# Twelve input projections between the memory's and the samples' attentions, in one program with a ring

## What is computed

```python
z = rmsnorm(x, norm_mix) @ w_in           # 6936 columns: 54 units of 128, and 24 for gates
o_lru = lru_branch(lru_x, lru_gate, ...)  # convolution, gates, recurrence over the tokens
o_nsa = nsa_attend(q, ...)                # compressed, selected and window keys, gated
o_mem = mem_attend(mq, mkv)               # softmax(mq mk / sqrt(128)) mv, 4 heads, 256 rows
z = merge0*(o_lru @ w_up_a) + merge1*(o_nsa @ w_up_b) + merge2*(o_mem @ w_up_m)
h = x + z @ w_o
y = h + (silu(f @ w_ffn_gate) * (f @ w_ffn_up)) @ w_ffn_down    # f = rmsnorm(h)
```

## Time and profile before

| | us |
|---|---|
| median of 3 runs (2675.41 to 2675.78) | 2675.66 |
| the profiled execution, device time | 2671.46 |
| its span, first to last instruction | 2669.8 |
| TensorE busy | 2416.7 (91%) |
| VectorE, ScalarE, GpSimd busy | 1072.0, 724.7, 655.0 |

### The profile page before, as it was taken

One profiled execution on the slowest core, in us unless ns is written; L12 is line 12 of the kernel. 1 busy time (PEld: TensorE's weight loads), 2 busy tenths in 40 slices (PEclk: granted clock), 3 DMA queues, 4 the chain that ended last, 5 costly groups with the idle time before them and its releaser, 6 DMA issues. The chain is left out here.

```text
span 2669.8 us, 37831 instructions
## 1 busy us (share of the span) xinstructions
PE 2416.7 (91%) x14415; PEld 2234.0 (84%) x14415; DVE 1072.0 (40%) x1945; ACT 724.7 (27%) x1319; POOL 655.0 (25%) x399
## 2 busy tenths in 40 slices
PE   7996877989989899899856587999999999999999
PEld 7995647789888788799733577999999999999999
DVE  5465014436255564655433003263333333333333
ACT  5222011242352544644332004232211111111111
POOL 2212001111111011010035001234444434433443
PEclk9997789999999899999678568999999999999999
DMA  5224424224233221110056626332111111111112
GB/s 178 88 80 168 125 72 147 67 67 128 64 97 88 74 63 52 60 49 28 6 125 181 160 65 246 104 119 91 61 48 47 40 47 47 47 39 47 47 47 79
DMA packets 136151, 226.26 MB, mean 85 GB/s; under 512 B 29418, under 2 KB 95098, under 8 KB 135420
## 3 DMA queue, kind: packets, MB, share of 16 engines
q1 hardware_dynamic: 122492, 194.57, 23.5%
q0 software_dynamic: 6560, 25.22, 3.2%
q10 hardware_dynamic: 6976, 4.79, 0.7%
HBM read 176.80 MB, written 55.08 MB: 87 GB/s over the span
## 5 line engine op out<-in xcount | busy, mean ns | idle before, releaser
L1101 PE MATMUL att_facc<-h_hi,att_w_hi 128*128 128x344 f32 x960 | 337.7, 352 | 57.8 <-DVE att_zf L1281 44.5
L2153 PE MATMUL tl_acc<-tl_x_hi,tl_w_hi 128*128 128x344 f32 x1632 | 348.0, 322 | 21.1 <-DVE tl_x_lo L2216 14.0
L2153 PE MATMUL tl_acc<-tl_x_lo,tl_w_hi 128*128 128x344 f32 x1632 | 347.2, 321 | 0.0
L2153 PE MATMUL tl_acc<-tl_x_hi,tl_w_lo 128*128 128x344 f32 x1632 | 345.4, 320 | 0.0
L1101 PE MATMUL att_facc<-h_lo,att_w_hi 128*128 128x344 f32 x960 | 314.5, 328 | 0.0
L1101 PE MATMUL att_facc<-h_hi,att_w_lo 128*128 128x344 f32 x960 | 314.2, 327 | 0.0
L2153 PEld LDWEIGHTS tl_acc<-tl_x_hi,tl_w_hi 128*128 128x128 f32 x1632 | 275.2, 189 | 22.5 <-issue 15.9
L2153 PEld LDWEIGHTS tl_acc<-tl_x_lo,tl_w_hi 128*128 128x128 f32 x1632 | 277.0, 189 | 0.0
L2153 PEld LDWEIGHTS tl_acc<-tl_x_hi,tl_w_lo 128*128 128x128 f32 x1632 | 272.6, 188 | 0.0
L2118 POOL TENSOR_TENSOR tl_w_lo<-tl_raw,tl_w_hi 128x1024 fp32r<-128x1024 f32 x64 | 153.9, 2404 | 425.1 <-ACT tl_w_hi L2059 425.1
L1101 PEld LDWEIGHTS att_facc<-h_hi,att_w_hi 128*128 128x128 f32 x960 | 187.7, 196 | 72.4 <-DVE att_zf L1281 42.2
(11 more groups left out here) (355 smaller groups left out, 4031.5 us busy)
## 6 DMA issues: line engine op xcount, KB each, us to landing
tl_raw<-in_w_ff SPq DMA_DIRECT2D x66, 512.0 KB, 3.6
z<-att_zf SPq DMA_DIRECT2D x120, 172.0 KB, 3.7
att_raw<-in_w_in SPq DMA_DIRECT2D x40, 512.0 KB, 4.3
tl_tmp<-z SPq DMA_DIRECT2D x24, 516.0 KB, 4.4
tl_raw<-in_w_up SPq DMA_DIRECT2D x16, 512.0 KB, 4.0
fr_raw<-in_w_in SPq DMA_DIRECT2D x14, 512.0 KB, 4.8
zn<-fr_x SPq DMA_DIRECT2D x10, 516.0 KB, 2.9
fr_x<-in_xT SPq DMA_DIRECT2D x8, 644.0 KB, 10.3
```

The lines of the kernel that those rows point to most:

```text
L1101: mm = pe.matmul(facc[:, 0:CW], w[:, u % 2, k, :], h[:, k, c * CW:(c + 1) * CW], start=(x == 0), stop=(x == 23))
L2153: mm = pe.matmul(a[:, c, 0:CW], wt[:, s, k, :], x[:, x0, c * CW:(c + 1) * CW], start=first and n == 0, stop=last and n == 2)
```

## The change

Twelve of the 24 `merge` units (42 to 53) leave the attention. Their 144 ticks are dealt among the items of a new program, `memory_and_samples`, that replaces the block of the three parts. The first two of them have their weights loaded and split at the end of the attention's order. The products of the samples' memory move: its scores stand between the group product and the transposes of the samples' attention, its values at the end. All keys and values of the samples come through one ring of ten slots of 512 KB, filled by the sync queue alone; weights of the twelve units and stores of their chunks go through GpSimd's queue. The 24 copies to the outputs move into the attention (items 24 to 47), on GpSimd's queue. The loops of the memory's attention become straight code, and the two products of new and compressed keys become one.

The diff, cut to its core:

```diff
+FILL = 12
 def attention_and_recurrence(...)
-    UNITS += list(range(U_MG, NU_IN))
-    NU = len(UNITS)
+    NU = len(UNITS) + NU_IN - FILL - U_MG
+    UNITS += list(range(U_MG, NU_IN - FILL + 2))
-    TICKS = ((4,),) * 3 + ((2, 2, 2, 1, 1) * 4 + (2,) * 4,) * (QT - 3)
+    TICKS = ((3, 2),) * 3 + ((2, 1, 1, 1),) * (QT - 3)
...
+                if 0 <= J - COPY < len(copies):
+                    dst, src, slow = copies[J - COPY]
+                    pool.dma_start(dst, src, allow_slow_non_contiguous=slow).then_inc(c_out, 16)
...
+def memory_and_samples(nc, d, per, h_hi, h_lo, fill):
+    DEAL = {"begin": 4, "mat": 2, "ks": 3, "grp": 2, "km": 1, "turn": 2, "vs": 3, "vm": 2}
...
+    ITEMS = []
+    for b in range(0, NS, 2):
+        ITEMS += [("ks", b), ("ks", b + 1), ("kw", b)]
+    ITEMS += [("km", b) for b in range(NS)]
+    for b in range(0, NS, 2):
+        ITEMS += [("vs", b), ("vs", b + 1), ("vw", b)]
+    ITEMS += [("vm", b) for b in range(NS)]
...
+            def ring_load(i):          # sync queue
+                kind, b = ITEMS[i]
+                slot, landed = ring[:, i % NR], r_in[i % NR]
+                if i >= NR:
+                    was, of = ITEMS[i - NR]
+                    read = {"k": mk_mm if was == "km" else k_mm, "v": mo_mm if was == "vm" else o_mm}[was[0]]
+                    sp.wait_ge(read, of + (2 if was[1] == "w" else 1))
+                if kind in ("ks", "vs"):
...
+                    with sp.Fori(0, PAGES) as x:
+                        page = sp.value_load(pt[0:1, bass.ds(x + b * PAGES, 1)], ...)
+                        sp.dma_start(slot..., src[bass.ds(page, 1)]...).then_inc(landed, 16)
...
+            for m in range(QT):
+                constants(m)
+                for i in range(loaded, min(NR, loaded + 2)):
+                    ring_load(i)
+                    loaded += 1
+                if m >= 2:
+                    o_store(m - 2)
+                if m + 2 < QT:
+                    q_load(m + 2)
+            o_store(QT - 2)
+            o_store(QT - 1)
+            for i in range(loaded, len(ITEMS)):
+                ring_load(i)
...
+            filler(("begin", 0))       # TensorE
+            pe.wait_ge(m_in, 32)
             scores(0)
             for j in range(NJ):
...
                 turn(j)
+                filler(("mat", j))
...
+            for b in range(NS):
+                sample_scores(b)
+                filler(("ks", b))
+            pe.wait_ge(s_oe, NJ)
+            pe.wait_ge(g_mm, 1)
+            pe.matmul(S5[0:RW, 0:NCMP], grp[:], lc[:, 0:NCMP], ...).then_inc(tp_done, 1)
+            filler(("grp", 0))
...
+            for b in range(NS):
+                memory_scores(b)
+                filler(("km", b))
+            pe.wait_ge(w_done, 1)
...
+            filler(("turn", 0))
+            pe.wait_ge(te_done, 4)
...
+            for b in range(NS):
+                sample_values(b)
+                filler(("vs", b))
...
+            for b in range(NS):
+                memory_values(b)
+                filler(("vm", b))
```

More of the change, by code:

```diff
@@ L1007, in _ @@
             q_low(0, 0)
-            for u in range(2, NU):
+            for u in range(2, NU + 2):
                 if unit_at[u - 2] == -1:
@@ new lines, in _, with filler @@
+        @block.tensor
+        def _(pe):
+            def filler(p):
+                for tick in ticks[p]:
+                    u, c, g, x0 = tick // 12, tick // 4 % 3, tick // 4, 6 * (tick % 4)
+                    if tick % 12 == 0 and u >= 2:
+                        pe.wait_ge(f_lo, u - 1)
+                    if x0 == 0 and g:
+                        pe.wait_ge(f_ev, g)
+                    for x in range(x0, x0 + 6):
+                        k = x // 3
+                        w, h = ((w_hi, h_hi), (w_hi, h_lo), (w_lo, h_hi))[x % 3]
+                        mm = pe.matmul(facc[:, 0:CW], w[:, u % 2, k, :], h[:, k, c * CW:(c + 1) * CW],
+                                       start=(x == 0), stop=(x == 23))
+                    if x0 == 18:
+                        mm.then_inc(f_mm, 1)
@@ new lines, in memory_queries @@
+            def memory_queries(part):
+                if part == 0:
+                    chain(dve.memset(mqb[:], 0.0))
+                    dve.wait_ge(mc_in, 16)
+                q0 = mqb[:].rearrange("p n c -> p (n c)")
+                for x in range(8 * part, 8 * part + 8):
+                    ins = dve.tensor_copy(q0[:, x * (RP + 1):x * (RP + 1) + 1], mqs[:, x % MH, x // MH:x // MH + 1])
+                if part == 3:
+                    ins.then_inc(mqb_done, 1)
+            evict(("begin", 0))
@@ new lines, in _ @@
+                if j:
+                    evict(("mat", j - 1))
+                if j == 16:
+                    sample_queries()
+                if j in (18, 20, 22, 24):
+                    memory_queries((j - 18) // 2)
+            evict(("mat", NJ - 1))
+            for b in range(NS - 1):
+                evict(("ks", b))
+            dve.wait_ge(k_mm, NS)
+            dve.wait_ge(b_in, 16 * 2 * NS)
+            chain(dve.tensor_copy(lc[:, 0:40], S3[0:RW, 2:42]))
+            chain(dve.tensor_tensor(lc[:, 40:NCMP], S3[0:RW, 42:2 + NCMP], b_cmp[:], ALU.add))
@@ new lines, in _ @@
+            dve.wait_ge(me_done, 1)
+            chain(dve.reciprocal(msc[:, 3:4], msc[:, 2:3]))
+            dve.tensor_scalar(mpr[:], mpr[:], msc[:, 3:4], None, ALU.mult).then_inc(mp_done, 1)
+            for b in range(NS):
+                evict(("vs", b))
+            dve.wait_ge(o_mm, NS)
+            for g in range(G):
+                rows = slice(g * HD, (g + 1) * HD)
+                dve.tensor_copy(soT[rows], S0[rows, 0:RW].rearrange("p (b h) -> p h b", h=8)[:, g * R:(g + 1) * R, :]).then_inc(o_done, 1)
```

786 lines of the change are left out of this document (391 added, 395 removed).

## The result

The changed kernel takes 2739.8 us against 2675.7: slower by 2.4% (ratio 1.0245, 95% interval 1.0208 to 1.0283). The prediction was 2666. Its profiled execution took 2735.85 us, with a span of 2734.2.

The account below looks back on a forecast made before the run. TensorE was taken to bound the prompt's attention, with holes in the stages behind it; -104 us there and +94 us in the second program give -10 us, from 2675.7 to 2666 us. Own range 2650 to 2684; with rivals 2635 to 2702.

Parts of the forecast that it names:

- The sum's sign: Whole kernel: attention -104 us plus second program +94 us gives -10 us, a faster kernel.
- The price of a removed tick: Attention: 108 ticks at 1.04 us and 40 at 1.15 us leave, giving back 112 and 46 us.
- the borders: Attention: 33 chunks ending in the middle of an item each wait 0.94 us for the eviction, 31 us.
- What comes back in waits: Attention: 31 us at chunk borders plus 21 us (10 for the recurrence's blocks, 11 for the next four tiles) return.
- The copies: Attention: the 24 copies to the outputs hide on GpSimd's queue and cost nothing.
- Memory's attention: Second program: 142.6 us instead of 76.5, +66 us, 18 of them waits for query tiles on the sync queue.
- Samples' scores, chain, first values: Second program: from the end of the memory's attention at 1490.4 us to the first values at 1572.8 us.
- Values: Samples' values: the sync queue is the bound at 24.9 us a pair of sequences; 86.7 us for the stage.
- rival 1: Second program: the gathers cost nothing on the sync queue, kernel 2617 us; chance 0.13.
- rival 2: Samples' values: the clock stays low, a pair takes 26.9 us and TensorE is the bound, kernel 2696 us; chance 0.22.
- Memory's values and the way into the tail: End of second program: 32.0 us for the memory's values with their ticks, then 16.3 us to the tail.
- Rival 3: Attention: more comes back, through a lower clock or late VectorE; gain only 78 us, kernel 2692 us; chance 0.22.

Follow-up runs that it names:

- e1: The changed kernel with ticks in the first three query tiles dealt so every chunk ends with its item: 2721.5 us, ratio 1.0162.
- e7: e6 with ticks 2, 1, 1 instead of 2, 1, 1, 1 in query tiles 3 to 7, so chunks end with items there too: 2640.9 us, ratio 0.988.
- e3: The changed kernel without the 24 copies to the outputs in the attention: 2759.6 us, ratio 1.0306.
- e2: The changed kernel with the second program's stores of memory outputs and query tile loads issued from ScalarE's queue: 2701.1 us, ratio 1.0115.
- e5: The changed kernel with the pages of values of sequences 1, 3, 5, 7 issued from ScalarE's queue: 2753.1 us, ratio 1.0291.
- e8: The new program with the queue edits of e2 and e5, but the twelve units back in the attention, no ticks in the second program: 2662.7 us, ratio 0.9963.
- e4: The changed kernel without the second program's 144 ticks (products, evictions and weights left out, stores of their size kept): 2678.3 us, ratio 1.0027.
- e6: The changed kernel with the edits of e1, e2 and e5 together: 2650.4 us, ratio 0.9904.
- e9: e7 with five ticks instead of three beside each sequence of samples' values, none beside the memory's values: 2624.8 us, ratio 0.9811.
- e12: The changed kernel run again, unedited, on another chip: 2749.4 us, ratio 1.0301.
- e13: The changed kernel with only the second program's ticks dealt as in e9: 2723.2 us, ratio 1.0184.

## Why the prediction was wrong, point by point

**The sum's sign.** -10 was predicted and +64 came: 47 us of the miss in the attention, 27 in the second program.

**The price of a removed tick: the step that failed.** I took the mean busy time of a tick, 1.04 and 1.15 us, as what a removed one gives back. The projections' busy time fell by 84.0 us for 108 ticks and by 34.3 for 40: 0.78 and 0.86 us a tick, 40 us less than the term of -158. A tick at the upper clock is six matmuls 0.157 us apart, 0.94 us; the prediction has this price, beside the row of bare chunks, and used it for the borders only. Part of the rest went back in the clock. In the first three tiles 76 of 1717 projection matmuls were at the lower clock before and 159 of 1069 after, each 0.13 us longer: 11 us; with the bank's borders aligned (e1) it is 118. Of the 28 us short there this explains 11 (0.10 us a tick) and 11; some 6 remain that I can't place. In the next four tiles the price alone explains 8 of the 12 us short (0.21 us a tick). The other products got 3 and 9 us longer in the two stretches, which I had not counted either.

**What comes back in waits** was right in sum: predicted 31 + 21 = 52 us, measured 33.6 + 16.8 = 50.4 us more time without work on TensorE. Its parts were not, so the agreement is luck. The short waits that I called borders (0.3 to 0.95 us) are 14 in the first three tiles, 10 us, and 4 in the next four, where I had counted 33; the long ones in the first three tiles grew from 15 to 44 us. I had put 25 us on borders there and 10 on the recurrence; e1 shows that both hang on where a chunk ends, and are worth 42 us together with the clock. In the next four tiles the waits moved from the eviction (19 to 9 us) to the transposes' copies (8 to 35 us); e7 took 13 us of these away by alignment, and that the recurrence's blocks hold the rest is argued, not tested.

**The copies** at nothing: right (e3).

**Memory's attention:** 142.6 predicted, 161.6 measured. An item without a disturbance took 3.37 us, less than my 3.75. That is 12 us less in all. The waits for transposes and the query tile were 44 us, not 18: this is the second step that failed. I went through the sync queue for the query tiles and missed the store in the same queue, for which ScalarE waits in front of its exponentials. Another 8 us are the lower clock (e2). Of the wait for tile 2 I had the size (4.1, it was 6.9). The wait of over 10 us that I announced for a later tile came, but for the store (e2).

**Samples' scores, chain, first values:** from the end of the memory's attention to the first values 83 us, predicted 82.

**Values:** 94.1 us, predicted 86.7 with the queue as the bound at 24.9 us a pair (it was 25.4). The pace was right, its explanation half: with the clock at 0.62 TensorE needed some 22 us of a pair, so it waited 3.6 us and not 11, and a second queue gave 9 us (e5), where rival 1 counts 31. This is most of rival 2: the clock did stay low, and my price of 26.9 us a pair for that was 5 too high. The Trainium skill (TensorE: Matmul & The Clock Gate, section HAM oscillation) lays a low clock to short bursts between waits; the traces here only half agree, since e5 and e8 have no such waits and a clock of 0.62 and 0.50.

**Memory's values and the way into the tail:** 32.0 and 17.0 (with the last two ticks in the first), predicted 32.0 and 16.3, in this profile. The terms given for the 32.0 add up to 30.8 only, and the size is luck: I had priced the memory's products at half clock, and this profile has the stage at 0.95. I had no case in which the ticks there run at half clock; other profiles have it, with 53 to 55 us.

**The rivals.** Rival 1 (gathers free) fell: in e4, without ticks, TensorE waits 12 us for each second sequence of values, and e2 alone is worth 49 us in its stage. Rival 3, the attention's low end of -78, had the right place and was too mild. All of my ends for the attention were built on 1.04 and 1.15 us a tick: with 0.94 us (19 us) and 12 us for the projections at the lower clock the sum would have been about +21, and with the 26 us of waits that I missed about +47. Nor does the forecast's own range follow from what it names: ends of -125 and -78 and 8 us either way are 2637 to 2700, not 2650 to 2684; the measured 2739.8 lies outside both.

## What to carry to other kernels

Price removed work at its marginal cost at full clock, not at the stage's mean; here even that was too much, as some of the rest then ran at the lower clock. When filling holes, align a fill chunk's end with the item it stands in, and keep a queue that moves long loops free of any store or load that an in-order engine waits for: follow every entry behind such a loop to its waiter, also the ones that free a buffer. And read what fill costs beside narrow products from more than one profile. Beside the samples' values a tick cost 1.3 us in e6's profile (84.7 - 54.3 of e8, over 24 ticks), 1.0 in e7's with the same code, and 1.0 in e9's (96.0 - 54.3 over 40). Beside the memory's values it cost 1.7 us where the clock stayed low (50.8 - 27.5 over the 14 ticks of the stretch) and next to nothing where it was up (27.7 in e12), since the narrow products then ran faster too.

## What the runs showed of the hardware

The granted clock stayed at 0.50 for 54 us in which TensorE was busy for 53.8, in products of 8 columns (e8); no wait but one of 1.4 us stands before them. In e9's values, of the 30 matmuls of 344 columns between two sequences 11 to 26 were 0.29 us apart, the first ones in five cases of seven, and the rest 0.16.

The same instructions without a wait took 27.7 us in one execution and 49.3 or 50.8 in others (a clock of 1.00 against 0.51 to 0.53). Without projections in that stretch the spread between runs of the changed kernel was 4 us (e13, four runs) instead of 32 (e12, six). What decides the level on entry is open.
